# Attention scores from stacked halves, normalisation on ScalarE, and a new order of the odd projection in a two-layer trunk step

## The reference

```python
def conformer_conv(u, conv_w, conv_b, ln_g, ln_b):
    val, gate = jnp.split(u, 2, axis=-1)
    g = val * jax.nn.sigmoid(gate)
    h = depthwise_conv(g, conv_w, conv_b, C_CONV // 2, C_CONV // 2)
    return jax.nn.silu(layer_norm(h, ln_g, ln_b))
...
    def one_block(qblk):
        s = jnp.einsum('bqhgd,bkhd->bhgqk', qblk, k, preferred_element_type=jnp.float32) * scale
        p = jax.nn.softmax(s, axis=-1).astype(v.dtype)
        return jnp.einsum('bhgqk,bkhd->bqhgd', p, v)
...
        u_s, q_s, k_s, v_s = odd_project(hs, od_w_in[li], q_norm[li], k_norm[li])
        q_s = apply_axial_rope(q_s, rope_cos, rope_sin)
        k_s = apply_axial_rope(k_s, rope_cos, rope_sin)
        k_all = jnp.concatenate([cache_k[:, li].astype(k_s.dtype), k_s], axis=1)
        att_s = block_attention(q_s, k_all, v_all)
        ys = odd_output(u_s, att_s, ...)
```

## Time and profile before

| What | Value |
|---|---|
| Runs | 2184.38, 2177.92, 2182.59 us; median 2182.59 |
| Profiled execution, own time | 2183.45 us |
| Its span (first to last instruction) | 2181.8 us |
| Mean granted clock of TensorE | 0.913 of 2.4 GHz |
| Busy: PE, DVE, ACT, POOL | 87%, 64%, 36%, 12% of the span |
| Odd projection; norm and rotary; attention | 832.4 to 930.8; 930.8 to 969.7; 969.7 to 1161.6 us |

### The profile page before, as it was taken

The page is one execution under the profiler, slowest core; times in us unless marked ns, Lnnn a source line. Parts: engine busy times, 40 slices in busy tenths (PEclk is TensorE's granted clock), DMA queues, the critical chain, the costliest instruction groups (busy, mean ns, idle before and its releaser), DMA issues.

```text
span 2181.8 us, 34451 instructions
## 1 busy us (share of the span) xinstructions
PE 1896.4 (87%) x11818; PEld 1676.3 (77%) x11819; DVE 1391.6 (64%) x2732; ACT 780.4 (36%) x1297; POOL 268.7 (12%) x280
## 2 busy tenths in 40 slices
PE   4898899999999999977789767979797898797975
PEld 2694599999999999933336646979687898797974
DVE  1578745678888854389875472448576796684435
ACT  1425333221222223323323332336444565452321
POOL 1001100000000000089300010020101110101021
PEclk9999899999999999956779987989898998898996
DMA  7343224457744424200000132467757898866433
GB/s 225 116 150 121 78 75 121 134 153 231 205 136 125 148 66 138 69 19 3 0 1 10 36 106 80 118 188 211 207 158 208 244 253 242 232 177 174 116 90 129
DMA packets 439501, 288.76 MB, mean 132 GB/s; under 512 B 20858, under 2 KB 428634, under 8 KB 439300
## 3 DMA queue, kind: packets, MB, share of 16 engines
q1 hardware_dynamic: 425124, 248.75, 39.4%
q0 software_dynamic: 12272, 34.50, 5.1%
q10 hardware_dynamic: 1904, 3.13, 0.5%
HBM read 262.86 MB, written 23.47 MB: 131 GB/s over the span
## 4 chain that ended last, share of the span: by engine, by line
PE 73%; DVE 14%; issue 8%; ACT 2%; DMA 1%; ACTq 1%; DVEq 1%; POOL 0%; POOLq 0%
PE ps L1116 15%; PE ps L1117 15%; PE ps L1118 15%; PE ps L1121 11%; PE ps L1122 5%; DVE vp L2105 3%; PE ps L1228 2%; DVE lo L1727 2%; PE ps L1159 1%; PE ps L1441 1%; PE ps L1178 1%; PE ps L1458 1%; DVE am L2166 1%; DVE hot L2320 1%; ACT hi L700 1%
## 5 line engine op out<-in xcount | busy, mean ns | idle before, releaser
L700 ACT ACTIVATE hi<-raw 128x1024 fp32r<-128x1024 f32 (+3 forms) x442 | 397.1, 919 | 512.9 <-PE ps L1118 348.3
L1116 PE MATMUL ps<-h_wide,hi 128*128 128x320 f32 (+1 forms) x1728 | 542.2, 314 | 32.6 <-issue 26.5
L1117 PE MATMUL ps<-h_wide,hi 128*128 128x320 f32 (+1 forms) x1728 | 537.5, 311 | 0.0
L1118 PE MATMUL ps<-h_wide,lo 128*128 128x320 f32 (+1 forms) x1728 | 537.4, 311 | 0.0
L1727 DVE TENSOR_TENSOR lo<-raw,hi 128x1024 fp32r<-128x1024 f32 (+3 forms) x442 | 451.9, 1050 | 48.3 <-ACT hi L700 44.1
L1116 PEld LDWEIGHTS ps<-h_wide,hi 128*128 128x128 f32 x1728 | 327.8, 190 | 35.3 <-issue 33.1
L1121 PE MATMUL ps<-h_wide,hi 128*128 128x256 f32 (+2 forms) x1056 | 294.2, 364 | 61.8 <-issue 54.6
L1117 PEld LDWEIGHTS ps<-h_wide,hi 128*128 128x128 f32 x1728 | 327.4, 189 | 0.4 <-issue 0.2
L1118 PEld LDWEIGHTS ps<-h_wide,lo 128*128 128x128 f32 x1728 | 327.6, 190 | 0.0
L1121 PEld LDWEIGHTS ps<-h_wide,hi 128*128 128x128 f32 x1056 | 210.7, 200 | 68.5 <-issue 52.6
L1122 PE MATMUL ps<-h_wide,lo 128*128 128x128 f32 (+2 forms) x1056 | 258.0, 244 | 0.0
(11 more groups left out here) (337 smaller groups left out, 2459.2 us busy)
## 6 DMA issues: line engine op xcount, KB each, us to landing
raw<-in_moe_w_dram SPq DMA_DIRECT2D x160, 512.0 KB, 5.2
raw<-in_w_mod_dram SPq DMA_DIRECT2D x96, 512.0 KB, 4.6
raw<-in_moe_w_dram SPq DMA_DIRECT2D x64, 384.0 KB, 3.5
raw<-in_ff_w_dram SPq DMA_DIRECT2D x40, 512.0 KB, 4.7
raw<-in_moe_w_dram SPq DMA_DIRECT2D x64, 320.0 KB, 3.8
y_rows<-zeros POOLq DMA_DIRECT2D x22, 512.0 KB, 4.5
raw<-in_moe_w_dram SPq DMA_DIRECT2D x32, 256.0 KB, 2.9
raw<-in_ev_w_in_dram SPq DMA_DIRECT2D x12, 512.0 KB, 6.4
```

The costliest lines, as they stand in the source:

```text
L700: act.activation(hi[c % 2][:, parts[h]], raw[slot][:, parts[h]], ACT.Copy).then_inc(hi_done, 1)
L1116: pe.matmul(out, w_hi, v_hi, start=first, stop=False, skip_group_check=True)
L1117: pe.matmul(out, w_hi, v_lo, start=False, stop=False, skip_group_check=True)
L1118: return pe.matmul(out, w_lo, v_hi, start=False, stop=last, skip_group_check=True)
```

## The change

There are four parts.

1. The odd projection runs in the order `ODD = (3, 5, 4, 6, 0, 1, 2)`: values and gates first, then q, k and v. Values are multiplied by gates (`gated`) after the third and the fifth pair, and 22 of the 93 taps are done between the evacuations. GpSimd's block may start when the fourth gating is done, after the fifth pair. SP loads the weights in the new order.
2. After the rotary turn q and k are split into high part and residue. `q_wide` and `q_tall` hold the high part of a head on 64 partitions and its residue on the other 64; `k_high` and `k_low` hold the same part of k on both halves. ScalarE writes copies, VectorE writes eight residues of q (64 x 512) and four of k (64 x 640). A score of a latent tile is then two fp32r products over a depth of 128, with `k_high` and with `k_low`. Context tiles stay as they are.
3. ScalarE normalises: `normed(s-1)` scales by the reciprocal that VectorE makes, between the exponential of s and the copy of s-2. VectorE's multiplication goes.
4. ScalarE copies all five transposed blocks at once; VectorE's copy of the fifth and its semaphore go. The norm gain of q takes in the factor -1/8, so scores are negated: VectorE takes a minimum, and the exponential takes it as its bias without a scaling between.

```diff
-MANY = [(ring_of(OIN + c), 3) for c in range(2)] + [(ring_of(OOUT + c), 1) for c in range(4)]
+ODD = (3, 5, 4, 6, 0, 1, 2)
+MANY = [(ring_of(OIN + ODD.index(c)), 3) for c in range(2)] + [(ring_of(OOUT + c), 1) for c in range(4)]
...
+        ptp = sin_t.rearrange("p (a c) -> p a c", a=4)
+        q_wide = place("q_wide", [P, 4, TS], F32R, at=at_spare)
+        q_keep = place("q_keep", [P, TS], F32R, at=at_rows)
+        at_qf = scratch + 4 * NC * (656 + 688)
+        q_tall = place("q_tall", [P, NC, T], F32R, at=at_qf)
+        k_high = [place(f"k_high{e}", [P, T], F32R, at=at_tmp + 4 * PADW * e) for e in range(2)]
+        k_low = [place("k_low0", [P, T], F32R, at=at_tmp + 8 * PADW), place("k_low1", [P, T], F32R, at=at_qf + 4 * T * (NC + 1))]
+        HEADS = [slice(0, HD), slice(HD, P)]
...
+            def odd_columns(c):
+                return q_columns(c) if c < 2 else columns(w, 2 * D_A + 512) if c == 2 else columns(w, (c - 3) * 256)
...
+            for p in range(2, 7):
+                load(OIN + p, odd_columns(ODD[p]))
...
+            for p in range(7):
+                split_hi(OIN + p + 2)
+                in_place(6 + p, ODD[p], z_odd)
...
+            for j in range(NC):
+                act.wait_ge(o_rope, j + 1)
+                act.activation(q_wide[HEADS[1], j, :], qf[HEADS[1], j, TP:T], ACT.Copy).then_inc(q_hi, 1)
+                if j:
+                    act.wait_ge(q_set, j)
+                act.activation(q_keep[HEADS[0], :], qf[HEADS[0], j, TP:T], ACT.Copy).then_inc(q_hi, 1)
+                act.wait_ge(q_lo, 2 * j + 2)
+                act.activation(q_tall[HEADS[0], j, TP:T], q_keep[HEADS[0], :], ACT.Copy).then_inc(q_set, 1)
+            act.wait_ge(o_rope, 5)
+            act.wait_ge(v_kept, 2)
+            for e in range(2):
+                for part in (e, 1 - e):
+                    act.activation(k_high[e][HEADS[part], :], kk[HEADS[e], :], ACT.Copy).then_inc(q_hi, 1)
...
-                    act.activation(pt[h % 2][:, 0:4, (t - 1) * P:t * P], ps[:, 4, 0:512].rearrange("p (k c) -> p k c", k=4),
+                    act.activation(pt[h % 2][:, :, (t - 1) * P:t * P], ps[:, 4:6, :].rearrange("p a b -> p (a b)")[:, 0:T].rearrange("p (k c) -> p k c", k=5),
                                    ACT.Copy).then_inc(a_kept, 1)
+            def normed(s):
+                width = P if s % TT == 0 else T
+                act.wait_ge(a_sum, s + 1)
+                act.activation(pp[:, s % 2, 0:width], pp[:, s % 2, 0:width], ACT.Copy, scale=am[:, 3, s % 2:s % 2 + 1]).then_inc(a_norm, 1)
...
-                    act.activation(dst, src, ACT.Exp, scale=HD ** -0.5, bias=am[:, 1, s % 2:s % 2 + 1],
+                    act.activation(dst, src, ACT.Exp, scale=-1.0, bias=am[:, 0, s % 2:s % 2 + 1],
                                    accum_out=am[:, 2, s % 2:s % 2 + 1]).then_inc(a_exp, 1)
+                if 1 <= s < NH * TT + 1:
+                    normed(s - 1)
                 if 2 <= s < NH * TT + 2:
                     kept(s - 2)
...
+                        e, rows = h // 4, slice((t - 1) * P, t * P)
+                        q = q_wide[:, h % 4, rows] if e else q_tall[:, h % 4, t * P:(t + 1) * P]
+                        pe.wait_ge(q_lo, 2 * NC + 4)
+                        pe.wait_ge(q_set, NC)
                         for i in range(2):
-                            last = pe.matmul(ps[:, 2 * (s % 2) + i, 0:TH], q, kk[r, i * TH:(i + 1) * TH], start=True, stop=True)
+                            cols = slice(i * TH, (i + 1) * TH)
+                            pe.matmul(ps[:, 2 * (s % 2) + i, 0:TH], q, k_high[e][:, cols], start=True, stop=False)
+                            last = pe.matmul(ps[:, 2 * (s % 2) + i, 0:TH], q, k_low[e][:, cols], start=False, stop=True)
...
+            dve.tensor_scalar(par[:, 1, QN:QN + 1], par[:, 1, QN:QN + 1], -HD ** -0.5, None, ALU.mult)
...
-            for c in range(7):
-                raw_out(6 + c, OIN + c, c, z_odd)
-                split_lo(OIN + c + 2)
+            def gated(c):
+                dve.wait_ge(in_kept, 2 * (6 + 2 * (c // 2 + 1)))
+                for lo_t, hi_t, cond in SEGS:
+                    p0 = (GC_P, GC_S)[cond]
+                    last = dve.tensor_tensor(gp[:, c, p0:p0 + hi_t - lo_t], gp[:, c, p0:p0 + hi_t - lo_t], vp[:, c, lo_t:hi_t], ALU.mult)
+                last.then_inc(gp_set, 1)
+            for p in range(7):
+                raw_out(6 + p, OIN + p, ODD[p], z_odd)
+                split_lo(OIN + p + 2)
+                if p in (2, 4):
+                    gated(p - 2)
+                    gated(p - 1)
+                if p >= 2:
+                    taps((4, 7, 4, 7, 0)[p - 2])
...
+            for j in range(NC):
+                dve.wait_ge(q_hi, 2 * j + 1)
+                dve.tensor_tensor(q_wide[HEADS[0], j, :], qf[HEADS[1], j, TP:T], q_wide[HEADS[1], j, :].bitcast(F32), ALU.subtract).then_inc(q_lo, 1)
+                dve.wait_ge(q_hi, 2 * j + 2)
+                dve.wait_ge(q_lo, 2 * j + 1)
+                dve.tensor_tensor(q_tall[HEADS[1], j, TP:T], qf[HEADS[0], j, TP:T], q_keep[HEADS[0], :].bitcast(F32), ALU.subtract).then_inc(q_lo, 1)
+            for e in range(2):
+                for part in (e, 1 - e):
+                    dve.wait_ge(q_hi, 2 * NC + 2 * e + 1)
+                    dve.tensor_tensor(k_low[e][HEADS[part], :], kk[HEADS[e], :], k_high[e][HEADS[e], :].bitcast(F32), ALU.subtract).then_inc(q_lo, 1)
...
-                        link(dve.reduce_max(am[:, 0, s % 2:s % 2 + 1], ps[:, 2 * (s % 2):2 * (s % 2) + 2, 0:TH], AX_XY))
-                    dve.tensor_scalar(am[:, 1, s % 2:s % 2 + 1], am[:, 0, s % 2:s % 2 + 1], -HD ** -0.5, None, ALU.mult).then_inc(a_max, 1)
+                        dve.tensor_reduce(low, ps[:, 2 * (s % 2):2 * (s % 2) + 2, 0:TH], AX_XY, ALU.min).then_inc(a_max, 1)
...
-                    link(dve.reciprocal(am[:, 3, u % 2:u % 2 + 1], am[:, 2, u % 2:u % 2 + 1]))
-                    dve.tensor_scalar(pp[:, u % 2, 0:width], pp[:, u % 2, 0:width], am[:, 3, u % 2:u % 2 + 1], None, ALU.mult).then_inc(a_norm, 1)
-                    dve.tensor_copy(pt[h % 2][:, 4, (t - 1) * P:t * P], ps[:, 5, 0:P]).then_inc(a_kept5, 1)
+                    if u >= 2:
+                        dve.wait_ge(a_norm, u - 1)
+                    dve.reciprocal(am[:, 3, u % 2:u % 2 + 1], am[:, 2, u % 2:u % 2 + 1]).then_inc(a_sum, 1)
```

More of the change, by code:

```diff
@@ L365, in hybrid_trunk_step @@
         a_exp = sem("a_exp")
+        a_sum = sem("a_sum")
         a_norm = sem("a_norm")
+        q_hi = sem("q_hi")
+        q_lo = sem("q_lo")
+        q_set = sem("q_set")
         a_t = sem("a_t")
         a_kept = sem("a_kept")
-        a_kept5 = sem("a_kept5")
         a_pv = sem("a_pv")
@@ L602, in q_columns @@
                      src[:, k:k + 4, e, 2 * c + j, :]) for k in (0, 4) for j in range(2) for e in range(2)]
-            for c in range(2):
-                load(OIN + c, q_columns(c))
+            def odd_columns(c):
+                return q_columns(c) if c < 2 else columns(w, 2 * D_A + 512) if c == 2 else columns(w, (c - 3) * 256)
+            for p in range(2):
+                load(OIN + p, odd_columns(ODD[p]))
             sp.wait_ge(evac, 2 * OIN)
@@ L612, in _ @@
             sp.dma_start(hspread[:, :, :], a["const_hspread"]).then_inc(odd_in, 16)
-            load(OIN + 2, columns(w, 2 * D_A + 512))
-            for c in range(3, 7):
-                load(OIN + c, columns(w, (c - 3) * 256))
+            for p in range(2, 7):
+                load(OIN + p, odd_columns(ODD[p]))
             wo = a["od_w_out"][0]
@@ L1834, in shift_lo @@
                 dve.wait_ge(n_shift, i + 1)
-                dve.tensor_tensor(sh_l, mod[:, layer, 24 * which:24 * which + KT, :], sh_h.bitcast(F32), ALU.subtract).then_inc(n_shift_lo, 1)
+                dve.tensor_tensor(sh_l, mod[:, layer, 24 * which:24 * which + KT, :], sh_h.bitcast(F32), ALU.subtract)
             def scaled_lo(i, layer, which, k):
@@ L1848, in raw_out @@
                     dve.wait_ge(in_kept, 2 * (n - 1))
-                bank = 4 * (c % 2)
+                bank = 4 * (n % 2)
                 for h in range(2):
@@ L2080, in z_odd @@
                 return gp[:, m - 10, p0 + lo_t:p0 + hi_t]
-            dve.wait_ge(gp_pads, 1)
-            for c in range(7):
-                raw_out(6 + c, OIN + c, c, z_odd)
-                split_lo(OIN + c + 2)
-            for c in range(NC):
-                if c % 2 == 0:
-                    dve.wait_ge(in_kept, 2 * (6 + 5 + c // 2 + 1))
-                for lo_t, hi_t, cond in SEGS:
-                    p0 = (GC_P, GC_S)[cond]
-                    last = dve.tensor_tensor(gp[:, c, p0:p0 + hi_t - lo_t], gp[:, c, p0:p0 + hi_t - lo_t], vp[:, c, lo_t:hi_t], ALU.mult)
-                last.then_inc(gp_set, 1)
             conv_w = GC_W - 30
@@ L2101, in taps @@
                     if j == 0:
-                        dve.wait_ge(gp_set, NC)
+                        dve.wait_ge(gp_set, c + 1)
```

(24 more changed lines are left out.)

7 lines of the change are left out of this document (removed).

## The result

The changed kernel took 2150.22 us (median of four runs, 2148.54 to 2161.71) against 2183.49 for the kernel before: ratio 0.9863, 95% interval 0.9824 to 0.9902. Run again it took 2161.34 (2143.67 to 2164.32) against 2181.48: 0.9896, 0.9866 to 0.9926. The profiled execution is one of 2149.14 us (span 2147.5).

A forecast was written before the change was run, and what follows sets the result against it. VectorE was taken to bind attention at 2.4 GHz, TensorE at 1.2 GHz and in the projection. 2183.45 + 16.5 (preparation) - 4.5 (opening) - 38.3 (heads) = 2157 us; own range 2146 to 2165.

The forecast's parts named there:

- ScalarE's loop as the new bound: Attention heads at 2.4 GHz: scores, normalising, copy, transposes and hand-overs close a loop of 3.2 us a step.
- exponential waiting for transposes: Attention heads: a sign of being right, ScalarE's exponential waits for TensorE's transposes, with steps near 3.2 us.
- The clock in the heads: Seven attention heads: half still have a 1.2 GHz stretch, +2.9 us each; 120 us instead of 158.3, so -38.3.
- (a): Rival, attention heads: the clock still drops at every head's end; heads 130 us, time 2167; chance 0.19.
- (c): Rival, attention heads: ScalarE's loop takes 4.0 us a step; heads 136 us, time 2177; chance 0.15.
- (d): Rival, attention heads: TensorE never regains 2.4 GHz after preparation and binds at 4.5 us; heads 163, time 2200; chance 0.10.
- New work ahead of the scores: After the rotary: twelve VectorE residues in turns with ScalarE's copies add 16.5 us, bounds 14 to 20.
- preparation beyond 20: Between rotary and scores: a sign of being wrong, making the halves of q and k takes over 20 us.
- Rival (b): Preparation after the rotary: VectorE's residues wait out GpSimd, 10 us more, time 2167; chance 0.08.
- Conv inputs first at nothing: Odd projection: 22 taps and eight gating products fit VectorE's free time under TensorE's 14.12 us pairs; cost nothing.
- The opening: Attention's start, before P·V runs: 23 us instead of 27.5, so -4.5.
- After attention 0: Everything behind attention: the same work, so a change of 0.

The follow-up runs named there:

- e5: The changed kernel with ScalarE normalising only the first 128 columns of P, leaving out part of the computation; 2154.96 us in its one run.
- e4: The changed kernel with GpSimd's column of the convolution started only when the halves of q and k are made; 2150.58 us, ratio 0.9876.
- e9: The changed kernel with float32 scores over 64 rows, no halves, and the projection's old order; 2157.79 us, ratio 0.9894; run again 2149.99 us, 0.9862.
- e3: The changed kernel with the normalising of P moved back from ScalarE to VectorE; 2169.16 us, ratio 0.9949.
- e7: The changed kernel with the residues of q taken inside the rotary stage, only the halves of k behind it; 2145.31 us, ratio 0.9832.
- e8: The changed kernel with q's residues inside the rotary stage and GpSimd's column started only behind the halves; 2144.78 us, ratio 0.9831.

## Why the prediction was right, point by point

- **ScalarE's loop as the new bound.** Right, in mechanism and size: 3.17 against 3.2, and e5 moved it by what was taken out. A head at 2.4 GHz is 15.8 (15.7 forecast). But not every step is this loop's: at the head's start the exponential waits for VectorE's minimum, and over the stage that is 30.0 of its 46.8 us of idle time. The sign "exponential waiting for transposes" came out in part.
- **The clock in the heads.** Half of the heads were to have a stretch at 1.2 GHz for 2.9 us each; in the first profile it fell before two of seven, for 2.0 and 1.4 us, in the second before three. The first head, which begins at 1.2 GHz beside GpSimd, is 3.4 us longer than 15.7, and the last, with fewer scores left to make, 1.9 shorter, which the forecast hadn't counted. Together 115.4 instead of 120. Rivals (a), (c) and (d) fell with it.
- **New work ahead of the scores.** The step that was mis-sized: 16.5 forecast, bounds 14 to 20, and 20.8 measured (21.7 less the 0.9 that was there before). That is beyond the bounds, and "preparation beyond 20" was one of the forecast's own signs of being wrong. What isn't residue was right, 4.9 us against 4.6. The twelve residues took 15.9 us (5.7 + 4.4 + 5.8 in the groups) where 8 x 0.935 + 4 x 1.1 = 11.9 were taken. The row of 0.935 came from a place where only half of the instructions were longer than alone (0.69 or 1.18); here eleven of twelve were. Rival (b) is right in kind: e4 puts GpSimd's share at 7.1 us, not at 10, and what stays without it, 13.7, is the lower bound's 14.
- **Conv inputs first at nothing.** Cost 1.0 us, by taps of 1.6 beside a GpSimd that started when it was forecast to; I had priced them with the mean of 0.989.
- **The opening.** 24.7 from the first minimum, 2.4 saved instead of 4.5: two taps beside GpSimd take 3.3 us there.
- **After attention 0.** The last head's own end gained 1.5 us. Of the other 10 the wait at a change of expert holds most; whose they are stays open, and they are larger than the errors above.
- **Sum to the last head:** 1.0 + 20.8 - 2.4 - 42.5 = -23.1 measured, 16.5 - 4.5 - 38.3 = -26.3 forecast. The errors of the preparation and of the heads nearly cancel, and that is luck; so is that the time came out 7 us below 2157 in the first series and 4 above it in the second, with a rest that varies by more.

What the prediction did not see is which edit earns it. It priced the cheaper scores and the moved normalising as one step. The table separates them in part: the normalising with the row minimum and the one copy gives 29.2 us (e9), the halves give back 2.7 to 7.1 of that, and the order is within 3.5 either way. Beside the halves the normalising itself is worth 8.7 us (e3). The row minimum and the one copy are in every changed kernel, so what they give alone no run shows, and how the 29.2 divide stays open. The halves pay only when their preparation lies under the rotary stage: to the last head e7 is 0.3 us and e8 4.5 us ahead of e9, which does without halves.

## What to carry to other kernels

When several edits come as one, price each against the bound that the others leave: once ScalarE's loop sets the long step, a cheaper product on TensorE earned 1.1 us a head at 2.4 GHz and 2 to 7 where the clock was low, and didn't pay for its preparation. Work that makes operands for a cheaper product is a stage of its own, so put it into the waits of the stage before, and not beside GpSimd. Parts that stay in every variant are never measured: leave each out once. And compare edits by landmarks of the stage when another stage's spread is as large as the effect.
